# A hybrid decoder layer on one core: 32x32 block transposes on VectorE in place of 48 TensorE transposes for states and tails

## What is computed

```python
h = x + 0.5 * swiglu(rmsnorm(x), w1g, w1u, w1d)                   # FFN1, 5632 wide
b, c, v, z, g_conv, g_pool = split(rmsnorm(h) @ w_in)
conv_y, conv_state = short_conv(c * v, conv_buf, conv_w)          # causal, width 3
pooled, pool_state = multiscale_pool(z, pool_buf)                 # windows 2, 4, 8, 16
merged = sigmoid(g_conv) * ((b * conv_y) @ w_conv_out) \
       + sigmoid(g_pool) * (pooled @ w_pool_group) * pool_scale
h = h + merged @ w_o
h = h + 0.5 * swiglu(rmsnorm(h), w2g, w2u, w2d)                   # FFN2
y = rmsnorm(h)
```

## Time and profile before

| | |
|---|---|
| median of 3 executions | 2774.57 us (2774.41 to 2775.44) |
| the profiled execution | 2774.16 us |
| its span, first to last instruction | 2772.3 us |
| granted TensorE clock, mean | 0.998 of full speed |
| TensorE busy | 2757.8 us, 99% |
| VectorE busy | 1537.4 us, 55% |
| ScalarE busy | 1052.8 us, 38% |
| GpSimd busy | 12.4 us |
| DMA | 412.27 MB, mean 149 GB/s |

### The profile page before, as it was taken

One profiled execution on the slowest core, in us unless ns is written; L12 is line 12 of the kernel. 1 busy time (PEld: TensorE's weight loads), 2 busy tenths in 40 slices (PEclk: granted clock), 3 DMA queues, 4 the chain that ended last, 5 costly groups with the idle time before them and its releaser, 6 DMA issues.

```text
span 2772.3 us, 47809 instructions
## 1 busy us (share of the span) xinstructions
PE 2757.8 (99%) x18725; PEld 2754.3 (99%) x18725; DVE 1537.4 (55%) x2166; ACT 1052.8 (38%) x1283; POOL 12.4 (0%) x22
## 2 busy tenths in 40 slices
PE   9999999999999999999999999999999999999998
PEld 8999999999999999999999999999999999999998
DVE  6555455554555585555555555575555555555555
ACT  5333333333333453333333334363333333333334
POOL 0000000000000000000000000000000000000000
PEclk9999999999999999999999999999999999999999
DMA  6444444444444445444444444454444444444443
GB/s 198 152 145 144 139 149 144 144 144 144 144 145 144 143 136 153 152 148 143 158 141 159 152 151 144 151 159 152 152 151 151 151 151 151 151 151 151 151 151 106
DMA packets 347876, 412.27 MB, mean 149 GB/s; under 512 B 13039, under 2 KB 283503, under 8 KB 347446
## 3 DMA queue, kind: packets, MB, share of 16 engines
q1 hardware_dynamic: 347264, 410.24, 46.9%
q0 software_dynamic: 560, 1.32, 0.2%
HBM read 408.42 MB, written 3.32 MB: 149 GB/s over the span
## 4 chain that ended last, share of the span: by engine, by line
PE 98%; ACT 1%; DVE 0%; issue 0%; DMA 0%; SPq 0%; ACTq 0%; DVEq 0%
PE bank L433 33%; PE bank L434 33%; PE bank L435 32%; DMA acc<-in_x_sample 0%; ACT tb L742 0%; PE bank L686 0%; ACT w_hi L702 0%; SPq L338 0%; DVE w_lo L957 0%; DVE tok L1029 0%; DVE xn_lo L1010 0%; ACT h L761 0%; DVE h L1126 0%; PE bank L660 0%; ACT acc L783 0%
## 5 line engine op out<-in xcount | busy, mean ns | idle before, releaser
L957 DVE TENSOR_TENSOR w_lo<-raw,w_hi 128x1024 fp32r<-128x1024 f32 x772 | 944.0, 1226 | 1021.9 <-ACT w_hi L702 1021.1
L702 ACT ACTIVATE w_hi<-raw 128x1024 fp32r<-128x1024 f32 x772 | 815.6, 1059 | 1322.3 <-PE bank L435 1321.3
L433 PE MATMUL bank<-xn_hi,w_hi 128*128 128x320 f32 (+2 forms) x4224 | 1314.3, 311 | 2.7 <-DVE xn_lo L1010 2.7
L435 PE MATMUL bank<-xn_hi,w_lo 128*128 128x320 f32 (+2 forms) x4224 | 1304.4, 309 | 0.0
L434 PE MATMUL bank<-xn_lo,w_hi 128*128 128x320 f32 (+2 forms) x4224 | 1303.4, 309 | 0.0
L433 PEld LDWEIGHTS bank<-xn_hi,w_hi 128*128 128x128 f32 x4224 | 793.0, 188 | 3.2 <-issue 3.1
L435 PEld LDWEIGHTS bank<-xn_hi,w_lo 128*128 128x128 f32 x4224 | 792.2, 188 | 0.0
L434 PEld LDWEIGHTS bank<-xn_lo,w_hi 128*128 128x128 f32 x4224 | 792.2, 188 | 0.0
L435 PE MATMUL bank<-hid_hi,w_lo 128*128 128x320 f32 (+1 forms) x1952 | 606.4, 311 | 0.0
L434 PE MATMUL bank<-hid_lo,w_hi 128*128 128x320 f32 (+1 forms) x1952 | 604.7, 310 | 0.0
L433 PE MATMUL bank<-hid_hi,w_hi 128*128 128x320 f32 (+1 forms) x1952 | 598.9, 307 | 0.4 <-issue 0.4
(11 more groups left out here) (109 smaller groups left out, 493.2 us busy)
## 6 DMA issues: line engine op xcount, KB each, us to landing
raw<-in_w_ffn_gate SPq DMA_DIRECT2D x176, 512.0 KB, 3.5
raw<-in_w_ffn_up SPq DMA_DIRECT2D x176, 512.0 KB, 3.5
raw<-in_w_ffn_down SPq DMA_DIRECT2D x176, 512.0 KB, 3.6
raw<-in_w_in SPq DMA_DIRECT2D x176, 512.0 KB, 3.5
raw<-in_w_conv_out SPq DMA_DIRECT2D x32, 512.0 KB, 3.9
raw<-in_w_o SPq DMA_DIRECT2D x32, 512.0 KB, 3.7
raw<-in_w_pool_group SPq DMA_DIRECT2D x4, 512.0 KB, 4.2
out<-acc SPq DMA_DIRECT2D x8, 256.0 KB, 3.1
```

The costliest lines, as they stand in the source:

```text
L433: pe.matmul(out, slot_hi(n, col, col + P), hi, start=start, stop=False)
L435: return pe.matmul(out, slot_lo(n, col, col + P), hi, start=False, stop=stop)
L702: act.activation(slot_hi(n), raw[:, n % RAW, :], ACT.Copy).then_inc(hi_done, 1)
L957: dve.tensor_tensor(slot_lo(n), raw[:, n % RAW, :], slot_hi(n).bitcast(F32), ALU.subtract).then_inc(lo_done, 1)
```

## The change

States and tails are turned by VectorE in blocks of 32x32. Such a transpose turns each block in its place within the 128 partitions, so the loads and stores put the four groups of 32 channels onto their four groups of 32 partitions, in pieces of 32 floats (128 bytes).

The buffers grow to whole blocks: `conv_past` and `ctail` to 16 x 32 columns, `pool_past` to 8 x 128, `ztail` to 8 x 96. The state rows are loaded into rooms of 512 and 1024 columns in the accumulators; the tails' rows lie in `pbuf`, which the merge leaves alone and the root of FFN2 (`rs`) uses again.

On GpSimd the two loads at the start go. Once FFN1's first block is through (`hid_lo_done` 4), four memsets clear the rooms (512, 1024, 512 and 768 columns), and 4 + 16 DMAs load the states. After the convolution 44 DMAs store the tails.

On VectorE two transposes of the states come in the last block of FFN1, at its chunk 1 (chunk 241 of all), behind a wait for the 20 loads. Two of the tails come between the convolution and the merge, behind waits for ScalarE's copies. Ahead of the root of FFN2 there is a new wait, for all 45 stores.

On TensorE the 48 transposes and their waits go, on ScalarE the nine copies out of PSUM.

```diff
-            pool.dma_start(conv_rows, state_conv.rearrange("l b w d -> (l b w) d")).then_inc(states_in, 16)
-            pool.dma_start(pool_rows, state_pool.rearrange("l b w d -> (l b w) d")).then_inc(states_in, 16)
             pool.memset(yconv, 0.0).then_inc(yconv_zero, 1)
...
-            pool.wait_ge(tail_rows, 6)
...
+            pool.wait_ge(hid_lo_done, 4)
+            for room in (conv_rows, pool_rows, ctail[:], ztail[:]):
+                pool.memset(room, 0.0).then_inc(room_zero, 1)
+            pool.wait_ge(room_zero, 2)
+            past = state_conv.rearrange("l b w (k g c) -> g (l b w) k c", g=4, c=32)
+            for g in range(4):
+                pool.dma_start(conv_rows[32 * g:32 * g + SEQS * CONV_PAST, :].rearrange("r (k c) -> r k c", c=32),
+                               past[g]).then_inc(states_in, 16)
+            past = state_pool.rearrange("l b w (k g c) -> g (l b w) k c", g=4, c=32)
+            room = pool_rows.rearrange("r (k b c) -> r k b c", b=4, c=32)
+            for g in range(4):
+                for b in range(4):
+                    n_rows = min(32, SEQS * POOL_PAST - 32 * b)
+                    pool.dma_start(room[32 * g:32 * g + n_rows, :, b, :],
+                                   past[g, 32 * b:32 * b + n_rows]).then_inc(states_in, 16)
+            pool.wait_ge(tail_rows, 2)
+            conv = ctail_rows.rearrange("r (k c) -> r k c", c=32)
+            pooled = ztail_rows.rearrange("r (k b c) -> r k b c", b=3, c=32)
+            for g in range(4):
+                pool.dma_start(new_conv_prompt[0, 0].rearrange("w (k g c) -> g w k c", g=4, c=32)[g],
+                               conv[32 * g:32 * g + CONV_PAST]).then_inc(tails_stored, 16)
...
+                for s in range(SEQS):
+                    b, r = divmod(POOL_PAST + 1 + STEPS * s, 32)
+                    steps = new_pool_sample[0, s, POOL_PAST - STEPS:POOL_PAST, :]
+                    pool.dma_start(steps.rearrange("w (k g c) -> g w k c", g=4, c=32)[g],
+                                   pooled[32 * g + r:32 * g + r + STEPS, :, b, :]).then_inc(tails_stored, 16)
```

```diff
             def sum_of_ffn1():
                 pe.wait_ge(spread_done, spr.at())
                 sum_squares(1, 4)
-                pe.wait_ge(states_in, 32)
-                for k in range(KD):
-                    last = pe.transpose(bank[5][:, 16 * k:16 * k + 16], conv_rows[:, k * P:(k + 1) * P],
-                                        ident[0:16, 0:16])
...
             def sum_of_mix():
                 sum_squares(2, 4)
-                pe.wait_ge(tails_done, KD)
-                for g in range(2):
-                    for k in range(4):
-                        last = pe.transpose(bank[2 + g][0:ZTAIL, k * P:(k + 1) * P], ztail[:, 4 * g + k, :], ident[:])
...
```

```diff
+            def turn_states(n):
+                dve.wait_ge(states_in, 16 * 20)
+                dve.transpose(conv_past[:].rearrange("p k c -> p (k c)"), conv_rows).then_inc(past_done, 1)
+                dve.transpose(pool_past[:].rearrange("p k c -> p (k c)"), pool_rows).then_inc(past_done, 1)
                 last = dict(work)
+                if next_norm == 1:
+                    last[1] = turn_states
...
             stage(N_CONV, CONV_TURNS, CONV_CHUNKS, (0, 4, 20, 4, 4, 12), conv_work)
+            dve.wait_ge(tails_done, KD)
+            dve.wait_ge(z_kept, 4)
+            dve.transpose(ctail_rows, ctail[:].rearrange("p k c -> p (k c)")).then_inc(tail_rows, 1)
+            dve.transpose(ztail_rows, ztail[:].rearrange("p k c -> p (k c)")).then_inc(tail_rows, 1)
...
+            dve.wait_ge(tails_stored, 16 * TAIL_STORES)
             rms_of_channels(2, 4)
```

## The result

The changed kernel takes 2791.09 us (2790.89 to 2791.63), the kernel before 2774.57: a ratio of 1.0059, interval 1.0046 to 1.0073. It is 16.5 us slower, where 4.3 us less were forecast and 2773.4 us was the end of the range. The profiled execution has a span of 2789.3 us against 2772.3.

The account below looks back on a forecast made before the run. TensorE, busy 2757.8 of 2772.3 us, was taken to bound the kernel. Gains of 1.08 (first sum), 2.04 (second sum) and 1.17 (start) sum to 4.29 us: 2774.57 becomes 2770.3 us, range 2768.9 to 2773.4.

Parts of the forecast that it names:

- First sum: At chunk 268: without the states' 24 transposes TensorE gains 1.08 us (1.01 to 1.16), with a new wait of 0.8 us.
- Second sum: At chunk 512: without the tails' 24 transposes TensorE gains 2.04 us (1.97 to 2.12), with a new wait of 0.5 us.
- Start: Ahead of TensorE's second chunk: GpSimd's memset starts earlier and frees VectorE's held tensor_scalar sooner; gain 1.17 us, bounds 0 and 1.21.
- VectorE's transposes: Ahead of the splits of chunks 245 and 416: 1.8 and 1.5 us taken, covered by VectorE's lead; cost 0.
- Pieces and stores: States' loads and tails' stores in small pieces, and the new wait ahead of FFN2's root: cost 0; loads' bounds 0 to 1.3 us.
- the gain stays: After chunk 268: TensorE wants chunk 271 0.7 us after VectorE has split it, so the first sum's gain isn't given back.
- a matmul pitch other than 0.155: Anywhere on TensorE: matmuls starting at another spacing than 0.155 us would show the prediction wrong.
- The rival with the full return: At both sums and the start: all of the transposes' time comes back, 5.60 us, 2769.0 us; 6%.
- the one with dear transposes: On TensorE: each of 48 transposes costs its 272 ns, 14.2 us with the start, 2760.3 us; 1%.
- the one with late stores: At VectorE's new wait ahead of FFN2's root: stores of 8 us each make chunk 512 11.8 us later, 2784.1 us; 4%.
- The rival with the held split: At the start: the memset holds VectorE's first split, TensorE's second chunk comes 1.83 us later, gain 1.29, 2773.3 us; 5%.
- The start that doesn't move: At the start: nothing is gained there, leaving 3.12 us in all, 2771.45 us; 10%.

Follow-up runs that it names:

- with 226: The changed kernel with 226 semaphore increments that no one waits for at the head of TensorE's program: 2806.54 us, 31 us of it at the start.
- the run with 16 increments: The changed kernel with 16 semaphore increments that no one waits for at the head of TensorE's program: 2769.79 us, timed again 2769.88 us, ratio 0.9984.

## Why the prediction was wrong

The terms, as the prediction put them:

- First sum, 1.08 us: 1.1 measured at chunk 268, with a wait of 0.79 us for `w_lo` where 0.8 was forecast; 0.1 of it is gone at the next chunk. Right.
- Second sum, 2.04 us: 1.8. The split starts 0.22 us behind the root, and I had put 0.04 there. The view names ScalarE's `w_hi` for it, but that was done near 1868.5, 0.9 us before the root's end at 1869.39, as the prediction had it. What lies between root and split in the trace are register operations of VectorE's own program (1869.42 to 1869.56); in the kernel before they ran while VectorE waited for ScalarE. Right in its mechanism, 0.2 us too much.
- Start, 1.17 us: 1.6 measured. The mechanism is shown by the two runs with the memset moved. The size was off since the memset began at 15.51 and not at 16.01, where GpSimd's first DMA stands in the kernel before: that issue starts 0.62 us behind the end of the semaphore wait ahead of it, the memset 0.07 us. So the tensor_scalar ended at 19.91, and TensorE's second chunk came without any idle time, 1.3 us earlier. The cap of 1.21 us that I set was too low too: another 0.3 us is gained within that chunk, where the matmuls behind the idle time had started further apart (23.12 to 23.36 in place of 0.15 us, and some ns each in the ones that follow; why isn't shown).
- VectorE's transposes: 0.70 to 1.2 us each, 3.6 us in all, near the low ends taken (3.3), and the cover of the first pair holds 5.1 us more; that of the second pair wasn't tried. Right.
- Pieces and stores: the cost of 0 is right, the price under it wasn't. I counted 8544 packets of 0.060 us, 18 us of all 16 engines for the states alone; queue q0 has 2080 packets in all, and those from the states' loads took 4.0 us of 16 engines and were down by 96 us, those of the stores 2.7 us, down by 1552. The 44 issues took 0.57 to 0.87 us each, not 0.51, with a lead of hundreds.
- That all of this leaves TensorE's other instructions as they were was not even written down as a step. It stood behind "the gain stays", behind the sum of three terms, and behind the list of what would show it wrong, which looks for waits in the merge's or FFN1's last block and not at a turn of a loop. (Its last sign, a matmul pitch other than 0.155, did show, as 0.27 behind the turns, but was not tied to a cause.) This is the step that failed. The change takes 49 instructions from ahead of a loop of 1578 instructions, and the loop slid by 49 places across a border of 256; the stops at its three turns cost 21.0 us, five times the gain.

Could the rows of before have shown it? The parts were there: the page has queue q8 with 34 packets of 16 KB, 8704 instructions at 256 each, where TensorE executed 38433; the packets stop during the convolution's later turns; and a count of the loop's instructions gives 6.2 blocks. That it begins 39 behind a border could be had from the packets only roughly. What the trace of before could not show is that eight blocks are one too many, since no loop of that kernel touches eight. It would have made a rival of its own, with a sign opposite to the forecast. In the runs here the bad beginnings are those from 2 to 25 ahead of a border, with 40 at the edge: by the loop's length (six blocks and 42 instructions) some 40 places of 256, one in six for a shift that is not counted.

The rival with the full return was refuted by the waits at chunks 268 and 512, the one with dear transposes by the same chunks, and the one with late stores by the time at which VectorE's root began (1865.13, after 0.85 us idle that the sum's two matmuls of 1864.31 ended, and not a store). The rival with the held split was refuted at the start: the memset began at 15.51, ahead of the split of 16.20, and that split lasted 1.23 us as before. The start that doesn't move was refuted by its 1.6 us. In the rival with late stores, 1860 less 1846.43 is 13.6 us and not 13.9; nothing hangs on it.

## What to carry to other kernels

An edit that adds or removes instructions of TensorE moves every loop behind it. Count the instructions of each loop and of what stands ahead of it, and see in the trace whether the instruction queue brings packets during the loop's later turns; if a loop of a little more than six blocks of 256 begins close ahead of a border, as here, a few idle instructions in a place where TensorE waits anyway can be worth more than the edit (22 us against 4.6 here). "issue" in the waits of the busiest engine, at the turn of a loop, with more packets on the instruction queue than before, is the mark of it; so is a branch that lasts microseconds in the trace.

A saving on the bound engine is capped by how far the next engine is ahead at that place; that cap was right to 0.2 us in both places.

## What the runs showed of the hardware that was not expected

- A TensorE loop of 1578 instructions is held when it touches seven blocks of 256 instructions and is brought anew at every turn when it touches eight. The price was 3.4 to 8.1 us a turn: the first stop 1.2 to 2.1 us (3.0 in the one turn with 226, 5.1 to 5.2 when both fall together), the second 0.3 to 2.9 us, and then matmuls at 1.2 GHz, 0.27 us apart and not 0.147, until the clock is granted in full again.
- The branch at such a turn lasted 3.6 to 4.4 us in the trace (5.4 in the one turn with 226), and 0.2 us where the loop was held.
- The wait view puts some of these stops down to VectorE ("DVE acc L1201", "DVE w_lo L938"), since that was the last semaphore in the matmul's wait; the run with 16 increments has the same VectorE work and none of the waits.
- One semaphore increment of TensorE's own sequencer took 0.15 us (31 us for 207).
- A VectorE tensor_scalar of 3 columns took 0.16 us alone, and 0.64 and 2.44 us when a GpSimd memset ran, ending 0.02 to 0.03 us after the memset each time.
- VectorE's 32x32 block transposes of float32 took 1203 ns for 1024 columns, 937 for 768 and 705 for 512: about 0.98 ns a column and 0.2 us.
